# Two elementwise sums and two adds of squares moved from VectorE and TensorE to GpSimd, and three weight splits moved ahead on ScalarE, in a two-layer encoder step

## The reference

```
x = x + 0.5 * _swiglu(_rmsnorm(x, norm_ffn1[i]), ffn1_w_in[i], ffn1_w_out[i])
u = _rmsnorm(x, norm_mix[i])
...                                   # mixer of the layer, x = x + y
x = x + 0.5 * _swiglu(_rmsnorm(x, norm_ffn2[i]), ffn2_w_in[i], ffn2_w_out[i])

def _swiglu(u, w_in, w_out):
    h = u @ w_in
    a, b = h[..., :D_FF], h[..., D_FF:]
    return (jax.nn.silu(a) * b) @ w_out
```

## Time and profile before

| | before |
|---|---|
| median of 3 runs | 1898.39 us (1894.95 to 1899.76) |
| the profiled execution, its own time | 1898.26 us |
| its span, first to last instruction | 1896.5 us |
| PE busy / PEld busy | 1872.6 us (99%) / 1849.8 us (98%) |
| DVE / ACT / POOL busy | 1253.8 (66%) / 866.4 (46%) / 329.1 us (17%) |

### The profile page before, as it was taken

One profiled execution on the slowest core, in us unless ns is written; L12 is line 12 of the kernel. 1 busy time (PEld: TensorE's weight loads), 2 busy tenths in 40 slices (PEclk: granted clock), 3 DMA queues, 4 the chain that ended last, 5 costly groups with the idle time before them and its releaser, 6 DMA issues.

```text
span 1896.5 us, 34433 instructions
## 1 busy us (share of the span) xinstructions
PE 1872.6 (99%) x13850; PEld 1849.8 (98%) x13850; DVE 1253.8 (66%) x1998; ACT 866.4 (46%) x1516; POOL 329.1 (17%) x352
## 2 busy tenths in 40 slices
PE   8999999999999999999999999999999999999998
PEld 7999999998999999999999999999989999999998
DVE  8874487668874488678853886453446888448843
ACT  7652355346552355345532553232334665235532
POOL 2210122121220122132201221300010322012112
PEclk9999999999999999999999999999999999999999
DMA  8763576334763576347644763221113576357632
GB/s 213 163 153 92 133 168 140 106 91 91 160 145 108 122 165 148 110 98 170 145 131 101 172 138 101 84 101 67 57 45 107 116 174 143 105 121 167 129 94 79
DMA packets 116830, 234.71 MB, mean 124 GB/s; under 512 B 13184, under 2 KB 15248, under 8 KB 116672
## 3 DMA queue, kind: packets, MB, share of 16 engines
q1 hardware_dynamic: 77440, 160.59, 28.0%
q0 software_dynamic: 38208, 69.42, 22.3%
q10 hardware_dynamic: 1024, 2.49, 0.4%
HBM read 228.92 MB, written 3.53 MB: 123 GB/s over the span
## 4 chain that ended last, share of the span: by engine, by line
PE 90%; DVE 4%; ACT 2%; DMA 2%; issue 1%; POOL 0%; DVEq 0%; ACTq 0%; POOLq 0%
PE ps L1829 48%; PE ps L1819 39%; DVE w_lo L1213 1%; DMA raw_y<-in_ffn_in 1%; DVE u L1267 1%; PE ps L2143 1%; PE ps L2209 0%; DMA raw_z<-in_ffn_in 0%; ACT w_hi L715 0%; PE ps L2146 0%; PE ps L2011 0%; PE ps L2133 0%; DMA x<-in_x 0%; PE ps L2118 0%; DVE rstd L1284 0%
## 5 line engine op out<-in xcount | busy, mean ns | idle before, releaser
L1829 PE MATMUL ps<-u,w_hi 128*128 128x288 f32 x4928 | 990.7, 297 | 12.8 <-DVE w_lo L1213 5.1
L1829 PEld LDWEIGHTS ps<-u,w_hi 128*128 128x128 f32 x4928 | 793.3, 189 | 18.0 <-DVE w_lo L1213 10.9
L1829 PE MATMUL ps<-u,w_lo 128*128 128x288 f32 x2464 | 729.0, 296 | 0.0
L1829 PEld LDWEIGHTS ps<-u,w_lo 128*128 128x128 f32 x2464 | 463.5, 188 | 0.0
L1819 PE MATMUL ps<-h_hi,w_lo 128*128 128x288 f32 x1386 | 298.0, 296 | 0.0
L1819 PE MATMUL ps<-h_hi,w_hi 128*128 128x288 f32 x1386 | 297.9, 296 | 0.0
L1819 PE MATMUL ps<-h_lo,w_hi 128*128 128x288 f32 x1386 | 297.8, 296 | 0.0
L715 ACT ACTIVATE w_hi<-w_raw 128x768 fp32r<-128x768 f32 (+3 forms) x164 | 136.1, 837 | 322.1 <-PE ps L1819 258.0
L1213 DVE TENSOR_TENSOR w_lo<-w_raw,w_hi 128x768 fp32r<-128x768 f32 (+3 forms) x164 | 167.8, 1032 | 163.1 <-ACT w_hi L715 160.9
L1819 PEld LDWEIGHTS ps<-h_lo,w_hi 128*128 128x128 f32 x1386 | 223.0, 189 | 0.0
L1819 PEld LDWEIGHTS ps<-h_hi,w_lo 128*128 128x128 f32 x1386 | 222.9, 189 | 0.0
(11 more groups left out here) (263 smaller groups left out, 2120.2 us busy)
## 6 DMA issues: line engine op xcount, KB each, us to landing
raw_a<-in_ffn_in SPq DMA_DIRECT2D x132, 256.0 KB, 3.8
w_raw<-in_ffn_out SPq DMA_DIRECT2D x64, 384.0 KB, 3.1
raw_y<-in_ffn_in SPq DMA_DIRECT2D x88, 256.0 KB, 3.5
raw_x<-in_ffn_in SPq DMA_DIRECT2D x88, 256.0 KB, 2.7
raw_x<-in_ffn_in POOLq DMA_DIRECT2D x88, 256.0 KB, 6.3
raw_y<-in_ffn_in POOLq DMA_DIRECT2D x88, 256.0 KB, 4.9
raw_z<-in_ffn_in POOLq DMA_DIRECT2D x88, 256.0 KB, 5.0
w_raw<-in_ffn_out SPq DMA_DIRECT2D x64, 320.0 KB, 3.1
```

The costliest lines, as they stand in the source:

```text
L1829: mm = pe.matmul(dst, w, m, start=prod in ("M1", "M2", "M5") and kp == 0 and p == 0, stop=kp == KP - 1 and p == 2, skip_group_check=prod i ...
```

## The change

Four edits, all at the start of `ffn_a` and `ffn_b`:

1. POOL adds pairs of squared tiles in place: for `ffn_a` tile 6 to 4 and 7 to 5, for `ffn_b` 5 to 4 and 7 to 6. PE multiplies six sums instead of eight tiles with the mean matrix.
2. POOL instead of DVE makes S2 for pairs 0 and 1 of `ffn_a`.
3. ACT, in `ffn_a`, squares all tiles and then makes the last part of `u7`, and splits M4 0 and M3 0 before it goes on to the copies of M5; in `ffn_a` and `ffn_b` it splits M5 2 before the two copies of M6. (These are A22 and S4 of pair 0 and S1 of pair 2.)
4. SP's loads of A21 for pairs 2 and 3 also wait until the low part of M5 of the pair before is made, since S2 no longer stands behind it on DVE.

```
             def load_a21(f, ph, n):
                 g = f.pair(ph, n)
+                if 2 <= g < 4:
+                    sp.wait_ge(lo_split, f.unit(ph, "M5", n - 2) + 1)
...
+            def make_s2(g):
+
+                pool.wait_ge(sums_made[1], 1)
+                pool.wait_ge(a11_landed[g], 16)
+                pool.wait_ge(s1_summed[g], 16)
+                pool.tensor_tensor(raw_z[g][:, :], raw_y[g][:, :], raw_x[g][:, :], ALU.add).then_inc(s2_summed, 1)
+
             def add_s3(f, ph, n):
                 g = f.pair(ph, n)
+                if g < 2:
+                    make_s2(g)
...
+            def add_squares(f, into, tile, made, sums):
+
+                pool.wait_ge(sq8_made, DT * f.i + made)
+                pool.wait_ge(sums_made[1], KP * f.i + sums)
+                pool.tensor_tensor(sq8[:, into, :], sq8[:, into, :], sq8[:, tile, :], ALU.add).then_inc(sq8_added, 1)
...
                 add_s4(f, ph, 1)
+                if ph == 0 and f is ffn_a:
+                    add_squares(f, 4, 6, 4, 3)
+                    add_squares(f, 5, 7, DT, KP)
+                elif ph == 0 and f is ffn_b:
+                    add_squares(f, 4, 5, 6, KP)
+                    add_squares(f, 6, 7, DT, KP)
                 add_s1(f, ph, 3)
...
                     if cold and (prod, n) == ("M2", 1):
-                        upto(f.unit(ph, "M1", 2))
+                        upto(f.unit(ph, "M5", 2))
                     elif cold and (prod, n) == ("M6", 0):
-                        upto(f.unit(ph, "M5", 2))
+                        pass
...
             square_tile(3)
-            u7_high(ffn_a, 3, 2)
             square_tile(5)
             square_tile(7)
+            u7_high(ffn_a, 3, 2)
+            upto(max(ffn_a.unit(0, "M4", 0), ffn_a.unit(0, "M3", 0)))
             ffn_in(ffn_a, 0, copied=2)
...
-                if SLOT[u] is None and prod == "M5":
+                if SLOT[u] is None and prod == "M5" and g >= 2:
...
+            def norm_inside(f, kp):
+
+                if f is ffn_a and kp == 1:
+                    norm_tile(f, 4, added=1)
+                    norm_tile(f, 1, made=5)
+                    norm_tile(f, 3, made=6)
+                elif f is ffn_a and kp == 3:
+                    norm_tile(f, 5, added=2, last=True)
+                elif f is ffn_b and kp == 1:
+                    norm_tile(f, 4, added=1)
+                elif f is ffn_b and kp == 3:
+                    norm_tile(f, 6, added=2, last=True)
```

More of the change, by code:

```diff
@@ L305, in encoder_step @@
     sq_last, sumsq_full, sq8_made = sem("sq_last"), sem("sumsq_full"), sem("sq8_made")
+    sq8_added = sem("sq8_added")
     mix_squared, mix_added = sem("mix_squared"), sem("mix_added")
@@ L1866, in norm, with norm_tile @@
                 mm.then_inc(norm_psum, 1)
[L1868 to L1877, removed]
+            def norm_tile(f, j, made=0, added=0, last=False):
+                if made:
+                    pe.wait_ge(sq8_made, DT * f.i + made)
+                else:
+                    pe.wait_ge(sq8_added, 2 * f.i + added)
+                for h in range(2):
+                    mm = pe.matmul(ps[:, 6 + h, 0:HALF], mean_w[:, :], sq8[:, j, h * HALF:(h + 1) * HALF],
+                                   start=made == 1, stop=last, skip_group_check=True)
+                if last:
+                    mm.then_inc(norm_psum, 1)
+            def norm_inside(f, kp):
[9 more added lines that the diff above has]
+                    norm_tile(f, 6, added=2, last=True)
             def ffn_in(f, ph):
@@ L1890, in ffn_in @@
                         if f is ffn_a:
-                            norm_tiles(f, range(2))
+                            norm_tile(f, 0, made=1)
+                            norm_tile(f, 2, made=2)
                         elif f is not ffn_b:
@@ L1903, in ffn_in @@
                         if order is COLD and products[0] == ("M6", 0):
-                            norm_tiles(f, ((2, 3), (4,), (5,), (6, 7))[kp] if f is ffn_a else (4 + kp,))
+                            norm_inside(f, kp)
                         elif f is ffn_b and ph == 0 and products[0] == ("M1", 0) and kp == 1:
                             pe.wait_ge(x_ready, 2 * DT + 6)
-                            norm_tiles(f, range(4))
+                            for i in range(4):
+                                norm_tile(f, i, made=i + 1)
                     seen.add(part)
```

## The result

The changed kernel takes 1903.83 us (median of 9 runs, 1900.56 to 1905.99); the kernel before, on the same chip, 1899.76 us (9 runs, 1894.95 to 1902.06). The ratio, estimated from all the runs, is 1.0023 with a 95% interval of 1.0014 to 1.0032: slower by 2.7 to 6.1 us (the two medians alone give 1.0021). The profiled execution took 1901.41 us.

A forecast was written before the change was run, and what follows sets the result against it. DVE's list was taken to bound the start of `ffn_a`, the S3 transfer that of `ffn_b`. 1898.26 + 2.64 + 0.55 = 1901.45, with 0.13 for the median 1901.6, stated as 1901.5 us; 8 in 10: 1896.5 to 1904.0.

The forecast's parts named there:

- What bounds the starts: In `ffn_a`, DVE's list up to the low part of A22 of pair 0 sets M5 of pair 2: 46.7 instead of 44.10.
- POOL's adds hold DVE: In `ffn_a`, each POOL add keeps out DVE's instructions with two SBUF inputs: two at 1.15 us, two at 1.23.
- The prediction's other estimate: In `ffn_a`, if each POOL add kept DVE out for all its length: 2 x 1.29 + 2 x 1.45 - 1.22 - 0.90 = 3.4 us.
- S2 off DVE, and ACT's order: In `ffn_a`, DVE's list loses 1.22 us of S2 sums and 0.90 us of standing for ACT's A22 split.
- Norm matmuls count nothing: In `ffn_a` and `ffn_b`, 3.44 us of saved PE work precede waits ended by something else, so they count nothing.
- SP's new wait: A21 loads behind the low part of M5, a split about 1 us later than now: no cost.
- `ffn_b`, +0.55: S2 and the S3 transfer come 1.10 us later; between nothing and 1.10 reaches the landing, the middle taken.
- The marks: About 0.3%, 5.7 us, as what a measurement can tell from no change: 1892.7 and 1904.1 us; within, 0.85.
- the main case: The forecast as summed, 1901.5 us, with its own range of 1899.5 to 1903.0 us; chance 0.66.
- DVE isn't held: In `ffn_a`, POOL's adds could begin where DVE stands for ACT: about 1.3 us less, 1897.0 us; chance 0.17.
- full queue: In `ffn_a`, the moved A22 load takes 7 us beside other transfers; DVE and PE wait 2.9 more: 1904.4; chance 0.09.
- The longer low clock: In `ffn_b`, PE waits about 0.5 us longer; three more microseconds at clock 0.50 give 1.5 us: 1903.0; chance 0.08.

The follow-up runs named there:

- act_only: The kernel before with ACT's new order (edit 3) alone, no add on POOL, S2 on DVE, eight norm tiles on PE: 1899.26 us, 0.9998 of before.
- idle_adds: `act_only` plus four POOL adds of two tiles of x at the change's places in `ffn_a`, results unused: 1902.13 us, 1.0021 of before.
- idle_writes: `act_only` plus four POOL writes of zeros at the same places in `ffn_a`, reading nothing, results unused: 1899.28 us, 1.0004 of before.
- squares_only: The changed kernel with S2 back on DVE and without edit 4; POOL's adds of squares and ACT's new order stay: 1901.63 us, 1.0014 of before.
- gap_filled: The changed kernel with 20 unused matmuls on PE in its wait ahead of M5 of pair 0 of `ffn_a`: 1903.82 us, 1.0023 of before.
- before_look: The kernel before, unchanged, executed and profiled once more: 1899.29 us.
- s2_only: The changed kernel without POOL's adds of squares, PE back on eight norm tiles; S2 on POOL and ACT's new order stay: 1901.69 us, 1.0014 of before.

## Why the prediction was right, and where it failed

- *What bounds the starts.* DVE's list in `ffn_a` was right for the change: of the +3.13 us in the list, +3.03 arrive at M5 of pair 2, over an A22 load of nearly unchanged length (4.04 us, 4.12 before). The prediction asked whether PE comes later than DVE there, and found rightly that it does not. But the margin is small: with the list of `act_only` PE comes last, as said above.
- *POOL's adds hold DVE.* Right as a mechanism, shown by `idle_adds` against `idle_writes`. **The step that failed is the size of this term**: 2.30 + 2.46 = 4.76 us was forecast, 5.30 measured. Three of the four came within 0.11 us of the forecast; the hold at 17.63 cost 1.89, not 1.15. The bound that I had set above, 1.45 us, was too low for it, and so is the 1.58 us that POOL's add itself took there. The prediction's other estimate, in which each add keeps DVE out for all of its length, gave 3.4 us for the list where 3.13 was measured; the sum gave 2.64.
- *S2 off DVE, and ACT's order.* 1.22 and 0.90 us forecast. The idle time was worth 0.99; S2's 1.22 agrees (two holds of 2.95 less 1.22 are 1.73, and 1.76 was measured). With the holds this makes 5.30 - 1.22 - 0.99 = +3.09 (measured +3.13) in place of +2.64. M5 of pair 2 was forecast at 46.7 and came at 47.24.
- *Norm matmuls count nothing.* Right for `ffn_a` in the change, where DVE is late; the table speaks against it where the list is shorter, though no run tried that alone. For `ffn_b` I had asked only whether the saving is hidden, and not when the sum would be ready: PE waits 2.42 us for it in a place where it did not wait before.
- *SP's new wait.* No cost of it shows: POOL's transfers for S1 of pairs 2 and 3, which need these loads, follow at 20.97 and 35.15 us without an idle time. It was not tried alone. (The code waits for M5 of pair n - 2, which last used the buffer, not for the pair just before.)
- *`ffn_b`, +0.55.* Not settled. Counted from the end of PE's first wait there (448.57 us; 446.29 before), S2's add came 0.92 us later than before where 1.10 was forecast, but the S3 transfer landed 1.39 us earlier, 23.29 instead of 24.68, as it took 5.15 us and not 7.46. The prediction was built on one execution of a transfer that takes from 5.76 to 7.62 us in kernels that do not touch it. In `squares_only` and `gap_filled` the clock fell to 0.50 for 3.4 us behind PE's new wait (from 461.7 and 462.2 us), PE did not wait in front of M5 of pair 2 at all, which the prediction had named as a sign of being wrong, and the last column is 0.9 us longer than in the change's own profile, where the clock did not fall. How often it falls in the timed runs is not known.
- *The marks.* The sum was +3.2 us over before, inside the measured 2.7 to 6.1. Yet I called it "no change": **the step from the sum to that verdict failed too**, because I had taken 0.3% as what a measurement can tell, from three runs that spread over 4.8 us. Nine runs a side told 0.23% from nothing, with 0.09% to either side. The median of 1903.83 lies above the range of the main case (to 1903.0) and at the upper end of the wide one; of that, 1.37 us is the kernel before, whose median was 1898.39 us in three runs and is 1899.76 in nine.
- *The rivals.* "DVE isn't held" fell with the rows at 15.96 to 32.86, "full queue" with the load of 4.04 us. The longer low clock was a rival for `ffn_b`; `gap_filled` rules it out for `ffn_a` alone, and in `ffn_b` it stays open (above).

Open is where the rest lies, if there is one. Up to `gate_two` the change costs 3.04 us in `ffn_a` against before and 3.46 against `before_look`; the measured +4.4 us are 0.9 to 1.4 more, but their interval, 2.7 to 6.1, takes both in. `ffn_b` can hold part of it; the spread there from one execution to the next, 31.94 to 33.62 for before alone, is larger than what is sought.

## What to carry to other kernels

An elementwise add that moves to GpSimd is not off VectorE if VectorE's list is full and made of instructions with two SBUF inputs: here each add of 512 to 576 columns took 1.06 to 1.89 us from VectorE, more than the 0.61 us that VectorE spent on making such a sum itself. Before matmuls are saved by a sum made elsewhere, look when the sum will be ready, not only whether the saving is hidden. Follow an engine's list to the next engine's work: here the next path in line, over PE, was so close that a gain of 0.99 us in the list gave 0.23 to 0.65 behind it. And where one transfer in one profile carries an argument, look at a second execution first.

## What was not expected of the hardware

- The hold at 17.63 is in the record although VectorE's instruction starts 0.44 us ahead of GpSimd's add (18.07): it ends at 20.27, 0.62 us after the add's end at 19.65, as if it had only begun then. It came again in `s2_only` (17.79 and 2.65 us) and `gap_filled` (17.52 and 2.66). So which of the two was issued first, on which the prediction's rule rests, can't be read from the starts of the records. Why an instruction that starts first is held was not tried.
- The hold works both ways. In `ffn_b` GpSimd's first add took 3.29 us instead of 1.45, beside two parts of VectorE that kept their 1.05 us each.
- The distances in VectorE's list repeat to 0.01 us between executions, whatever the clock of TensorE and the first loads do; the total time of the same kernel spreads over 7 us (1895.57 to 1902.75 in 33 runs), and in these runs it falls by about 1.2 us for each 0.001 that the mean granted clock is higher (0.992 to 0.997; correlation -0.83). Where a list decides, its distances tell what a change did far more finely than the total; what follows the list repeats less well (28.33 and 27.91 us to `gate_two` for before).
